# Writing the rest of the weights over the loaded chunk, and loading behind TensorE

## The reference

```python
proj = rmsnorm(x, norm_mix_w) @ w_in          # 2048 x 7168
x = x + mix @ w_out                           # 2048 x 2048
mq = rmsnorm(x, norm_mem_w) @ w_mq            # 2048 x 2048
mk_mv = rmsnorm(mem, mem_kv_norm_w) @ w_mkv   # 2048 x 4096
x = x + m_o @ w_mo                            # 2048 x 2048
u = causal_dwconv(rmsnorm(x, norm_ffn_w) @ w_up, conv_w, conv_b)   # 2048 x 11264
a, b = jnp.split(u, 2, axis=-1)
x = x + (jax.nn.silu(a) * b) @ w_down         # 5632 x 2048
...
y = concatenate([y_a, y_b, y_c]) @ w_out_2    # second block: w_in_2, w_out_2, w_up_2, w_down_2
```

## Time and profile before

| | |
|---|---|
| median of 3 runs | 2656.85 us (2656.82 to 2657.67) |
| profiled execution, its own time | 2656.91 us |
| its span, first to last instruction | 2655.1 us |
| PE busy (matmuls) | 2645.5 us, 100% |
| DVE busy | 1785.3 us, 67% |
| ACT busy | 1341.5 us, 51% |
| loads of weights, SP queue | 899 whole chunks of 512 KB, 4.3 us median to landing |
| granted clock of PE | 0.999 in the mean |

### The profile page before, as it was taken

One profiled execution on the slowest core, in us unless ns is written; L12 is line 12 of the kernel. 1 busy time (PEld: TensorE's weight loads), 2 busy tenths in 40 slices (PEclk: granted clock), 3 DMA queues, 4 the chain that ended last, 5 costly groups with the idle time before them and its releaser, 6 DMA issues.

```text
span 2655.1 us, 41674 instructions
## 1 busy us (share of the span) xinstructions
PE 2645.5 (100%) x15689; PEld 2333.1 (88%) x15689; DVE 1785.3 (67%) x2180; ACT 1341.5 (51%) x1638; POOL 149.8 (6%) x106
## 2 busy tenths in 40 slices
PE   9999999999999999999999999999999999999999
PEld 9888888889999888888888889998888888888887
DVE  7677567555645777777775456998777777776444
ACT  6554365464533655555553344444665555554443
POOL 2001200000200200000001222000020000000000
PEclk9999999999999999999999999999999999999999
DMA  7555455546544555555555555555555555556554
GB/s 261 192 159 184 142 182 182 176 154 199 177 135 160 183 194 188 188 189 190 188 189 189 190 189 177 191 190 173 167 191 190 189 188 187 187 189 207 191 192 148
DMA packets 256256, 487.12 MB, mean 183 GB/s; under 512 B 15069, under 2 KB 80629, under 8 KB 255616
## 3 DMA queue, kind: packets, MB, share of 16 engines
q1 hardware_dynamic: 254496, 476.11, 53.8%
q0 software_dynamic: 1488, 9.19, 1.0%
q10 hardware_dynamic: 144, 0.01, 0.0%
HBM read 483.12 MB, written 2.13 MB: 183 GB/s over the span
## 4 chain that ended last, share of the span: by engine, by line
PE 94%; DVE 4%; ACT 1%; POOL 1%; issue 0%; DVEq 0%; ACTq 0%; POOLq 0%
PE ps L2087 94%; DVE w_lo L1311 1%; DVE acc L1834 1%; POOL sumsq L719 1%; ACT w_hi L779 0%; DVE ya L1898 0%; DVE x_res L2068 0%; DVE ua L1345 0%; ACT lnz L1205 0%; PE ps L2618 0%; PE ps L2405 0%; DVE y_lo L1376 0%; DVE ya L1900 0%; DVE cvp L1888 0%; DVE ya L1894 0%
## 5 line engine op out<-in xcount | busy, mean ns | idle before, releaser
L1311 DVE TENSOR_TENSOR w_lo<-raw,w_hi 128x1024 fp32r<-128x1024 f32 x899 | 1120.2, 1248 | 792.5 <-ACT w_hi L779 791.5
L2087 PE MATMUL ps<-op,w_hi 128*128 128x512 f32 (+1 forms) x6208 | 1639.9, 354 | 0.1
L779 ACT ACTIVATE w_hi<-raw 128x1024 fp32r<-128x1024 f32 x899 | 949.4, 1059 | 1111.1 <-PE ps L2087 1096.1
L2087 PEld LDWEIGHTS ps<-op,w_lo 128*128 128x128 f32 x5024 | 948.6, 189 | 170.2
L2087 PE MATMUL ps<-op,w_lo 128*128 128x256 f32 x5024 | 1090.1, 279 | 0.0
L2087 PEld LDWEIGHTS ps<-op,w_hi 128*128 128x128 f32 x6208 | 955.2, 190 | 5.0 <-issue 2.8
L2087 PE MATMUL ps<-g,w_hi 128*128 128x512 f32 x704 | 219.6, 393 | 0.0
L2087 PE MATMUL ps<-w_hi,g 128*128 128x512 f32 x704 | 217.7, 390 | 0.0
L2087 PE MATMUL ps<-w_hi,op 128*128 128x512 f32 x512 | 163.5, 394 | 0.0
L2087 PEld LDWEIGHTS ps<-g,w_lo 128*128 128x128 f32 x704 | 132.4, 188 | 30.0
L2087 PEld LDWEIGHTS ps<-w_hi,g 128*128 128x128 f32 x704 | 132.2, 188 | 30.2
(11 more groups left out here) (309 smaller groups left out, 1525.5 us busy)
## 6 DMA issues: line engine op xcount, KB each, us to landing
raw<-in_weights SPq DMA_DIRECT2D x899, 512.0 KB, 4.3
x_res<-in_x SPq DMA_DIRECT2D x8, 256.0 KB, 5.7
mem_x<-in_mem POOLq DMA_DIRECT2D x1, 2048.0 KB, 8.6
x_res<-in_x POOLq DMA_DIRECT2D x1, 2048.0 KB, 8.6
w_row<-row_dram POOLq DMA_DIRECT2D x2, 1024.0 KB, 6.8
out_x<-x_res SPq DMA_DIRECT2D x3, 512.0 KB, 2.9
rel_rev<-rel_dram POOLq DMA_DIRECT2D x1, 1024.0 KB, 8.0
hg_con<-in_hg_consts POOLq DMA_DIRECT2D x1, 576.0 KB, 5.4
```

The costliest lines, as they stand in the source:

```text
L779: nc.scalar.activation(w_hi[:, s], raw[:, s], ACT.Copy).then_inc(hi_rounded, 1)
L1311: TT(w_lo[:, s], raw[:, s], w_hi[:, s].bitcast(F32), ALU.subtract).then_inc(chunk_split, 1)
L2087: return nc.tensor.matmul(out, lhsT, rhs, start=start, stop=stop, skip_group_check=True)
```

## The change

`w_lo` no longer has memory of its own: it is placed at the address of `raw`, with the same shape. DVE's subtraction then reads `raw[:, s]` and `w_hi[:, s]` and writes its result over `raw[:, s]`. The memory of `raw[:, s]` is now read by PE's matmuls, so SP may load a new chunk into it only when PE has used the old one. All five waits of SP before a load change from `chunk_split` to `chunk_used`, with the same count. The other tiles move down by the 16 KB per partition that become free.

```diff
+        raw_at = at[0]
         raw = place("raw", [P, SLOTS, CW])
         w_hi = place("w_hi", [P, SLOTS, CW], F32R)
-        w_lo = place("w_lo", [P, SLOTS, CW], F32R)
+        w_lo = place("w_lo", [P, SLOTS, CW], F32R, offset=raw_at)
...
             def first_block(c):
                 if c >= SLOTS:
-                    sp.wait_ge(chunk_split, c - (SLOTS - 1))
+                    sp.wait_ge(chunk_used, c - (SLOTS - 1))
...
                     for s in range(SLOTS):
-                        sp.wait_ge(chunk_split, SLOTS * i + s - (SLOTS - 1))
+                        sp.wait_ge(chunk_used, SLOTS * i + s - (SLOTS - 1))
...
-                            sp.wait_ge(chunk_split, g.first_chunk + 2 * g.chunks * i + (n - (SLOTS - 1)))
+                            sp.wait_ge(chunk_used, g.first_chunk + 2 * g.chunks * i + (n - (SLOTS - 1)))
...
-                        sp.wait_ge(chunk_split, n - (SLOTS - 1))
+                        sp.wait_ge(chunk_used, n - (SLOTS - 1))
...
-                sp.wait_ge(chunk_split, g.first_chunk + n - (SLOTS - 1))
+                sp.wait_ge(chunk_used, g.first_chunk + n - (SLOTS - 1))
```

## The result

The changed kernel takes 2725.4 us in the median of four runs (2724.1 to 2729.4) against 2657.1 for the kernel before (2656.8 to 2657.7): a ratio of 1.026, with a 95% interval of 1.0249 to 1.0272. It is 68 us slower; the forecast was 2708, its range 2680 to 2745.

The account below looks back on a forecast made before the run. The prediction took PE's matmuls as the bound (busy 2645.5 of 2655.1 us). Removed work was worth 0; late loads 7.5, results behind splits 17.9 and bursts 25.3 added 50.7 to 2656.9, giving 2708 us, range 2680 to 2745.

Parts of the forecast that it names:

- the way held likeliest: Whole kernel: late loads, results behind a split and bursts add up, giving 2693 to 2725 us; chance 0.55.
- rival 3: PE's clock falls to half after each of three long stalls, adding 12 us: 2720; chance 0.1.
- bursts: Stretches where an engine's work between two splits exceeds a beat (out_2, attention, conf, pool, gated and others): 25.3 us lost.
- Lead afterwards: How early a chunk's w_lo is ready before PE needs it: 1.2 us in `up`, 2.4 with landings of 3.4.
- Rival 2: In the big products the ring of buffers becomes the bound as landings slow: 2720 to 2840 us; chance 0.1.
- Rival 4: No loss: loads land in 3.1 us everywhere and the lead covers nearly all places, 2657 to 2662 us; chance 0.05.
- Late loads: Slow landings beside `mem`, beside down_2's weight row, in the first block and elsewhere make PE wait: 7.5 us.
- The first block's two terms: In the first block, a load landing in 7.7 us costs 1.9 us, and the very first operand pairs about 3.
- Results behind a split: Results PE needs soon, queued on ACT or DVE behind a chunk's rounding or subtraction, come late: 17.9 us.
- The root: End of the first block: `root(0)`, behind the rounding of chunk 18, comes late and leaves PE standing 4.8 us.
- Pairs 4 and 7 of `up`: Head of `up`: operand pairs made by DVE behind a later split come 2.6 and 3.5 us late, 6.1 together.
- Rival 1: Only the work itself counts: existing waits swallow later starts, so attention, conf and part of the silus drop out: 2683; chance 0.2.

Follow-up runs that it names:

- experiment 1: The changed kernel with w_lo given its own memory again, SP's five waits kept on chunk_used: 2725.9 us, ratio 1.0266 to the kernel before.
- experiment 2: The changed kernel with eight raw buffers, still written in place, loading n when n-8, n-6, n-5 or n-4 is used: 2657.2, 2657.1, 2660.7, 2717.9 us.
- experiment 5: The changed kernel with the 176 loads of `up` held back one chunk more, until PE has used n-3: 2806.4 us, ratio 1.0563 to the kernel before.
- experiment 3: The changed kernel, one move each: root a chunk earlier 2718.4 us; PE's sums in up and up_2 a chunk later 2717.4; `up` operand pairs a chunk earlier 2718.8.
- the control: The changed kernel with eight raw buffers and SP's loads written out, chunk n still loaded when PE has used n-4: 2717.9 us, ratio 1.0222 to the kernel before.
- the three moves together: The changed kernel with root a chunk earlier, sums a chunk later and down_2's second weight row loaded in eight pieces: 2708.7 us, ratio 1.0194 to the kernel before.

## Why the forecast was right, and where its sum was short

The mechanism was right: the steady state keeps a lead, and places with something queued behind a split pay. The time, 2725.4, lies just above the 2693 to 2725 of the way held likeliest and nearer to rival 3's 2720; it is inside the whole range. That the sum fell only 17 us short is partly luck, since its bursts were some 8 us too high and made up for part of the places it missed.

**The cycle and the steady state.** "The lead today is 5.96 us" was 5.95; "Lead afterwards 1.2 in `up`, 2.4 with 3.4" was 1.0 at a median landing of 4.8, and 2.7. "So the removed work is worth 0": shown by experiment 1 and by the eight-behind kernel of experiment 2. "The steady state costs 0 as long as the lead stays positive": true down to a lead of 0.34 us and not to 0. The late chunk of each block, for which 0.3 to 0.5 us were forecast to be left, has from 0.05 to 1.2 (in most blocks under 0.6) and costs 1.7 us in `up` and 2.6 in `up_2`. Rival 2 (the ring as the bound) falls with the unbroken beat; experiment 5 shows what it would have looked like, one beat further on. Rival 4 (no loss) falls with the result, and needs one beat more, as experiment 2 shows. One reading was wrong and entered no term: SP's old release came not "about four beats earlier" than the new one but 8.7 us, 3.1 beats (median in `up`).

**Late loads, 7.5 us.** The row's load, 2.4: measured 2.7. The load beside `mem`, 2.6: it landed in 8.5 us, but PE waited for something else. DVE's split of that chunk ended in time, and behind it stood da_k's two steps and the masked copy of 2.54 us for which PE stood 3.7 us; with the half-clock stretch the place costs 5.5. One load of 8.4 us beside POOL's 1 MB load of rel_rev, at 91 us, was not in the sum: 2.7. The trace before has its like (7.5 us at 81.3). Another, of 7.2 us beside POOL's first weight row at 1803.8, costs 1.4 in gated; 7.2 + 2.57 - 8.36 is 1.4 too, so the formula held and the place was missed, and the trace before has 6.5 us there. A load of 8.8 us in the trace before (391.9), beside POOL's second load of `x`, was left out of the sum too; its like took 8.6, and PE did not stand for it. The first block's two terms, 1.9 and 3, came to 1.6 together. The 6.4 us of the earlier trace rows, 0.6, did not come again: no load landed later than 6 us there.

**Results behind a split, 17.9 us.** The mechanism held wherever it was applied, and the three moves of experiment 3 show it singly. The root: 3.8 of wait and 1.7 of clock against 4.8; its chunk landed in 4.4 us and not in 5.3, which is nearly the whole difference of the wait. Pairs 4 and 7 of `up`: 2.50 and 2.52 of wait, 6.7 with one stretch of half clock, against 6.1. The smaller places (heads of hg_g and `up`, out, mem_o) 3.7 against 4. What failed is the search for such places. The gather ahead of the sums in `up` and up_2 (3.9 and 2.6 us, the first with a stretch of half clock), POOL's sums of squares and DVE's query pairs in mem_q (3.2), the pairs at the head of up_2 (3.4 with its first chunk) and the last four chunks of down_2, which PE goes through twice and so releases late (3.5), have the same form and stood in no term: 16.6 us with the stretch of half clock among them.

**Bursts, 25.3 us.** out_2: 8.1 measured, 9.3 forecast. Attention: 5.7 in mem_k and mem_v, forecast 6. conf, pool and gated: 2.4, forecast 5, all of it in gated, and 1.4 of it is the late load above. "Then out 3": nothing beyond the 0.9 counted above. "The first two products 2": 1.9 in da_fm, nearly all of it where PE waits for `v_hg`, which ACT reads out. Here the sum was some 8 us too large. Rival 1 (only the work itself counts) said that the attention would drop out, and it did not.

**The clock.** Rival 3 was priced at 12 us for three stretches; it is 5 stretches of 1.7 us, 8.5. It was put down as another way in which it could go, but it belongs in the sum beside the likeliest one. The sign "PE's busy time stays" failed with it and with the restarts: it grew by 21.1 us. Where stalls of some 3 us are forecast, the clock must be priced with them.

Together: places forecast cost 42 us against 50.7, places missed 23 (the 16.6, the loads beside rel_rev and the first weight row, and the 2.6 of late chunks in up_2), small ones in `up` 2; in these are 8.5 us of half clock, and the 0.3 us of each restart, which the forecast nowhere had. The balance of the three is what puts the time 17 us above the forecast.

## What to carry to other kernels

When a buffer's release moves to a later engine, the steady state can be nearly free and the kernel still slower: the lead that was thrown away is what covered each result, mask, root or gather queued behind the feed's instructions on the same engines. Work out the lead that is left in beats of the bounding engine, then go through every wait of that engine that has anything queued behind a feed instruction, not only those for the feed itself, and compare its room with the lead lost; price a stall at its length plus a restart (0.3 us here), plus the clock, and count a lead under 0.34 us as a loss too. Here loading one chunk earlier (at n-5) kept all but 4 us of the 68, and two earlier all of it; both were run with eight buffers, which is all the memory of before, and a ring of just five or six, which would still free 12 or 8 of the 16 KB, was not tried.

## What the runs showed of the hardware that was not expected

- A half-clock stretch is 3.4 us long here, and in six of the ten traces that have any, one of them is 6.8. The length of a wait does not tell whether one comes. In these ten traces it came with all 17 waits of 3.3 us or more, with some from 1.8 us on, and not with one of 3.07; the wait of 2.85 us at 1872 was followed by one in the changed kernel, one of 2.89 at 2001 was not. With the root moved forward its own stretch was gone, and another stood at 96.4 us behind a wait of 2.0; the trace had eight in all instead of five. This is part of why four runs of one such kernel spread by 5 to 17 us, where the kernel before, with next to no stall, spreads by under 2: the control's fastest and slowest runs, 2706.4 and 2723.8, had mean granted clocks of 0.998 and 0.994, which is an estimated 11 of the 17 us.
- The same load of 512 KB at the same beat has two levels of landing, about 3.7 and 4.8 us, and stays at one of them for tens or hundreds of chunks: in `up` the median was 4.8 in the changed kernel, 3.7 with the pairs moved, 3.8 in the control with four behind. Medians of 16 chunks in `up` of the kernel before lie between 4.2 and 4.7. What chooses the level was not found. The Trainium skill (DMA: Bandwidth & Descriptors, section Anatomy of one DMA — SWDGE (gpsimd) path) gives 2.0 us plus bytes over 436 GB/s for POOL's path, an estimate of 3.2 us; neither level on SP's queue is as short as that. It is worth 1 us of lead, and it is seen in the time by stage: with the sums moved, `up_2` lost 2.7 us in the trace that had the lower level all through it, and 5.9 in the one of the three moves together, where its median was 4.8.
- Beside a 1 MB load by POOL the slowest load of 512 KB landed in 7.7 to 8.5 us, and the two behind it in 4.8 to 7.0, in the nine traces where the loads ahead of it were at the higher level; in the three at the lower level the slowest was 5.6 to 7.2 (the second weight row, loaded whole). In pieces of 128 KB the slowest was 5.7.
- PE loses about 0.3 us at a chunk whose w_lo is complete only as PE gets to it, even if its matmuls show no gap; it takes 0.34 us of lead to lose nothing.
- A subtraction that writes over one of its inputs takes the 1.225 us of one that doesn't.
